# The order of the mixed matrices' steps within a tile of the convolution stage: masks before shares on DVE, first share before multiply on GpSimd

## What is computed

```
xbc = silu(dwconv(xbc, conv_w, conv_b))          # 24 tiles of 128 channels; 16 of them xs, 4 B, 4 C
cb  = einsum('bclgn,bcsgn->bcgls', Cc, Bc)       # the "likeness" of a unit (c, g): 128 x 128
Lm  = exp(where(lower, a_cs[l] - a_cs[s], -inf)) # the "fall", one per head and direction
y_diag = einsum('bcgls,bcgrls,bcsgrp->bclgrp', cb, Lm, x)   # uses cb * Lm * dt
```

## Time and profile before

| what | us |
|---|---|
| median of 3 runs | 3413.67 |
| lowest, highest | 3412.81, 3415.64 |
| the profiled execution: its own time | 3416.97 |
| its span (first to last instruction) | 3415.1 |
| PE busy in it | 3049.4 (89%) |
| DVE, ACT, POOL busy | 1096.8, 547.6, 319.0 |

### The profile page before, as it was taken

One profiled execution on the slowest core, in us unless ns is written; L12 is line 12 of the kernel. 1 busy time (PEld: TensorE's weight loads), 2 busy tenths in 40 slices (PEclk: granted clock), 3 DMA queues, 4 the chain that ended last, 5 costly groups with the idle time before them and its releaser, 6 DMA issues. The chain is left out here.

```text
span 3415.1 us, 37508 instructions
## 1 busy us (share of the span) xinstructions
PE 3049.4 (89%) x15486; PEld 1604.7 (47%) x15486; DVE 1096.8 (32%) x2359; ACT 547.6 (16%) x1073; POOL 319.0 (9%) x262
## 2 busy tenths in 40 slices
PE   6998999988899998999999999987977889996986
PEld 5444744645444445634434443434537753544332
DVE  2232802677643012201101101112166553523113
ACT  2001700455012001000000000002022312301111
POOL 0003000255720000000000000000002200001001
PEclk9998999999999998999999999998988989997997
DMA  7721021353312224499999999996010031054996
GB/s 272 253 99 50 2 78 37 112 167 105 108 65 99 74 74 192 202 423 427 428 427 428 427 428 428 427 428 233 22 37 2 3 123 42 18 229 148 423 425 258
DMA packets 141423, 702.21 MB, mean 206 GB/s; under 512 B 18667, under 2 KB 46990, under 8 KB 108233
## 3 DMA queue, kind: packets, MB, share of 16 engines
q1 hardware_dynamic: 124601, 663.80, 48.7%
q10 hardware_dynamic: 11616, 27.92, 2.2%
q0 software_dynamic: 5040, 8.13, 0.7%
HBM read 697.32 MB, written 22.68 MB: 211 GB/s over the span
## 5 line engine op out<-in xcount | busy, mean ns | idle before, releaser
L2151 PE MATMUL ec_wide<-ec_ring,ec_xg 128*64 128x512 f32 x2048 | 454.7, 598 | 16.5 <-issue 12.3
L2151 PEld LDWEIGHTS ec_wide<-ec_ring,ec_xg 128*64 128x64 f32 x2048 | 146.8, 137 | 304.1 <-issue 299.9
L2185 PE MATMUL ec_acc<-ec_ring,ec_hidT 128*64 128x512 f32 x1024 | 235.1, 614 | 32.6 <-DMA ec_ring<-in_w_exp_down 31.8
L2310 DVE TENSOR_SCALAR ec_xg<-ec_piece,ordered 128x128 f32<-128x128 f32 x64 | 21.9, 405 | 567.7 <-PE ec_piece L2199 567.7
L2185 PEld LDWEIGHTS ec_acc<-ec_ring,ec_hidT 128*64 128x64 f32 x1024 | 82.2, 141 | 182.6 <-issue 182.3
L2892 POOL TENSOR_TENSOR solve_T<-const_rw,solve_T 128x512 f32<-128x512 f32 x8 | 10.1, 1265 | 1305.9 <-DVE solve_T L2930 1305.9
L2199 PEld LDWEIGHTS ec_piece<-ec_sel,x 128*128 128x128 f32 x512 | 122.9, 336 | 8.6 <-issue 5.7
L2199 PE MATMUL ec_piece<-ec_sel,x 128*128 128x128 f32 x512 | 124.4, 405 | 2.8 <-DVE ec_sel L2292 2.8
L3850 PE MATMUL hm_gu<-hm_ring,hm_xg 128*64 128x512 f32 x432 | 118.8, 616 | 6.1 <-DMA hm_ring<-in_moe_w_gu 3.4
L2274 ACT ACTIVATE ec_hidT<-ec_acc 128x512 f32<-128x512 f32 x32 | 17.4, 594 | 514.1 <-PE ec_acc L2174 514.1
L1255 PE MATMUL conv_main<-hT,conv_early 128*128 128x512 f32 x192 | 86.2, 604 | 2.9 <-DVE bcT L1365 2.9
(11 more groups left out here) (663 smaller groups left out, 5009.4 us busy)
## 6 DMA issues: line engine op xcount, KB each, us to landing
ec_ring<-in_w_exp_gate SPq DMA_DIRECT2D x64, 2048.0 KB, 18.5
ec_ring<-in_w_exp_up SPq DMA_DIRECT2D x64, 2048.0 KB, 27.0
ec_ring<-in_w_exp_down SPq DMA_DIRECT2D x64, 2048.0 KB, 19.7
hm_ring<-in_moe_w_gu SPq DMA_DIRECT2D x27, 2048.0 KB, 25.0
hm_ring<-in_moe_w_down SPq DMA_DIRECT2D x11, 2048.0 KB, 29.5
ahead_qkv<-in_w_in SPq DMA_DIRECT2D x10, 2048.0 KB, 9.4
hm_ring_late<-in_moe_w_down SPq DMA_DIRECT2D x5, 2048.0 KB, 25.4
u2T<-in_moe_w_gu SPq DMA_DIRECT2D x5, 2048.0 KB, 23.7
```

Of the source, the lines that this page charges most:

```text
L2151: last = pe.matmul(wide[half(e), b, :], xg[:, u % 2, j, half(e)], w[e][:, a, b * 512:(b + 1) * 512], start=(j == 0), stop=(j == KD - 1))
L2185: last = pe.matmul(acc[half(e), h, :], hidT[:, f, half(e)], w[e][:, r, h * 512:(h + 1) * 512], start=(f == 0), stop=(f == FT - 1))
L2310: last = dve.tensor_scalar(xg[:, u % 2, j, :], piece[:, m % 2, i * P:(i + 1) * P], scale_cols[:, j:j + 1], shift_cols[:, j:j + 1], ALU.mul ...
```

## The change

Two orders change; no instruction is added or removed. On DVE `share_back` no longer comes ahead of the masks for the units of the tile before, but at the end of the tile, for the same tile's units. On POOL `share_ahead` of tile i comes first, then `mix` of the units of tile i - 1, then `fall_together`; only behind a tile with two units does `mix` still come first (both share buffers are in use then).

```diff
@@ POOL @@
             for i in range(N_TILES):
-                for u in alike_at(i - 1):
-                    mix(u)
+                behind = len(alike_at(i - 1)) < 2
+                if not behind:
+                    for u in alike_at(i - 1):
+                        mix(u)
+                for u in alike_at(i):
+                    share_ahead(u)
+                if behind:
+                    for u in alike_at(i - 1):
+                        mix(u)
                 for u in falls_at(i):
                     fall_together(u)
-                for u in alike_at(i):
-                    share_ahead(u)
@@ DVE @@
             for i in range(1, N_TILES):
                 conv_main(i)
-                for v in alike_at(i - 1):
-                    share_back(v)
                 for n_at, v in enumerate(alike_at(i)):
                     mask_alike(i, n_at * P, v)
                 conv_side(i)
                 for v in falls_at(i):
                     ...
                     ahead_falls(v)
+                for v in alike_at(i):
+                    share_back(v)
```

## The result

The changed kernel took 3421.71 us (median of 9 runs, 3420.92 to 3424.27) against 3415.64 for the kernel before, run beside it. The ratio is 1.0022 (95% interval 1.0012 to 1.0032): slower by 6.1 us by the medians, by 7.5 by the ratio. The direction and the range of the prediction held; the size was between half and two thirds of the +11.7 forecast.

What follows compares the result with a forecast made beforehand. It took a loop through ACT, POOL and DVE, 13.07 us a tile, as the bound, with no engine full. Terms 0.6 + 14.6 - 3.5 gave +11.7 us on 3413.67, so 3425 us; range 3412 to 3434 (8 in 10).

Steps and rivals of the forecast that it cites:

- the landing loses its cover: Between POOL's fall and the next share_ahead: the store's landing, 5.3 to 6.0 us, loses its earlier 6.6 us of cover.
- DVE and POOL shut each other out: On the shared access: share_back always meets mix, its first instruction taking about 2.4 us.
- DVE goes first where both wait: At the turn after mix: share_back passes first, fall_together is shut out until then and takes some 4.2 us.
- the second rival: On POOL, the fall goes ahead of the waiting share_back: period 12.9 to 14.7 us, about no change, 3414 us; chance 14%.
- a chain that I had called covered: ACT's chain behind conv_side, 3.85 us, ends at 2.1 of the next tile, ahead of the fall at 6.3.
- The term 9 x 1.62: Nine tiles, 12 to 21, each 1.62 us longer (14.7 instead of 13.08): 14.6 us slower.
- the likeliest case: Convolution stage at a period of 14.5 to 14.9 us a tile: 3419 to 3431 us; chance 68%.
- The ends: Stretch up to tile 12, with the two-unit tiles, +0.6 us; tiles 21 to 23 at the far end, -3.5 us.
- PE's wait: PE's wait for the masks ahead of its side products: about 3.3 us a tile instead of 1.64.
- PE's clock: Rival: PE's idle time lowers its clock; deciding only with the whole tile at 1.2 GHz (22.9 us), over 3480 us; 2%.
- the covered 14.3 of 14.7: PE's work a tile with part at the lower clock, 11.44 + 2.86 = 14.3 us, still fits in the 14.7 period.

Runs made afterwards that it cites:

- e1: The changed kernel with SP issuing a unit's store ahead of the backward-row load instead of behind it: 3399.0 us, ratio 0.9953 against the kernel before.
- e9: Changed kernel with each unit multiplied in its own tile and ACT's decay ahead of back_falls, store still behind the row load: 3427.43 us, ratio 1.0041 against the kernel before.
- e6: The kernel before with two added POOL multiplies of 128x512 behind each share_ahead of units 4 to 15: 3431.06 us, ratio 1.0044.

## Why the prediction was half right

*That the landing loses its cover* was right in place and price: `share_ahead` waits for the DMA 8 times, the landing of the store issued at 757.40 took 5.3, within the 5.3 to 6.0 used; e1 removes the wait (and the stalls that came with it) and about 20 us, each against the kernel before beside it (-13.8 and +6.1), and e9 brings it back without any stall.

*That DVE and POOL shut each other out* was right: first `share_back` instruction 2.43 as forecast (2.4), and e6 prices it one to one.

*That DVE goes first where both wait* is the step that failed. I took from the earlier trace rows that the whole `share_back` would pass ahead of the fall. One instruction passes, the one that `mix` had held; then POOL's step, asked for earlier, takes its turn. So the fall is not delayed in that kind of tile (2.40, not 4.2), the store leaves 1.9 earlier than I had it (6.96 behind the share's start instead of 8.9), and the next share comes 12.57 behind the last.

That is the second rival, to which I gave 14%. It also had the other kind of tile in outline: the next share finds `ahead_falls` behind it to shut out. What I had not worked out is what follows in that tile. The fall waits 1.95 for ACT's rows, a chain that I had called covered, and then for the rest of `share_back`, and the next share comes 15.78 later. The rival's range of 12.9 to 14.7 a tile holds the measured average of 14.06; the value that I took from it, 13.5 and so 3414 us, was too low. The term 9 x 1.62 measured 9 x 0.99 = 8.9. That the time still fell into the likeliest case's own 3419 to 3431 is luck in part: the landing and the shared access were priced rightly, the turn between the fall and `share_back` was not.

*The ends* (+0.6 and -3.5) measured +1.1 and -3.1. The first is two errors that nearly cancel. The share ahead of tile 12 came at 705.84, 1.6 earlier than the 707.4 I had, and unit 4's share had not waited for a store at all; but then `share_back` took 6.36, as it also met the fall, and `conv_main` followed 8.2 behind the share instead of 6.2. *PE's wait* I had at 3.3 in each tile; it comes in every second, at 2.7 to 4.7, in sum 24.9 against 26.2 before.

*PE's clock*: the wait of 4.29 in the timeline of PE was followed by `side` at 6.62, with a granted clock of 0.76 over the stretch, so between the two levels in the mean (columns as in the earlier trace rows):

```profile
747.09 6.62 PE L1270 MATMUL conv_side<-hcT,conv_late 128*128 128x256 f32 x16 [4.29 <-DVE y L1421]
```
```profile
740.00:754.00 14.00, 9.71 (x28) 6.60 (x27) 13.71 (x33) 5.40 (x14) 6.06 (x4) 0.76 0.35 112
```

Still PE ended ahead of need: no steady tile had `conv_main` waiting for PE, as the covered 14.3 of 14.7 had it. No run here takes the clock away by itself.

## What to carry to other kernels

When steps are put in another order, write down for each buffer what releases it and where that release now falls: here the store of the shares had 6.6 us of cover because it was needed a round later, and a queue that issues it behind an unrelated wait turned that cover into the period. Then lay the engines that share an access path side by side in time; DVE work with one input from PSUM is the place for POOL's steps (2.04 beside one and without). A stall in the loop is paid in full (1.61 gave 1.62), one off the loop is free (1.24 gave nothing), and a gain may need several moves that each lose alone: the SP order by itself +0.17%, POOL's +0.27%, the two together -0.39%.

## What the hardware showed that I had not expected

Turns between DVE and POOL went, in every case looked at here, to whoever had asked first, not to one of the engines. A POOL step asked for while eight DVE instructions run back to back waits through all of them (3.83 for a step of 2.36 in the changed kernel, and 4.24 in the earlier trace rows). A DVE instruction held up by a POOL step passes when that ends, but the second one is held again if POOL's next step was already asked for (2.43 and 2.43). Between two POOL steps that follow each other one DVE instruction gets through, so each step holds one instruction more: two multiplies of 1.04 each (2.16 in all) stalled DVE by 1.61.
